# Conditioning weights scaled on ScalarE and summed on VectorE, and six more gate jobs by seven products

## What is computed

```python
# first stack                                   # second stack
g, u = jnp.split(h @ w_up[i], [D_FF], -1)       m = jax.nn.silu(c) @ ada_w[i] + ada_b[i]
g = depthwise_conv_centered(g, ffn_conv_w[i],   shift1, scale1, gate1, shift2, scale2, gate2 = split(m, 6)
                            ffn_conv_b[i])      u = causal_dwconv(h @ w_up, conv_w, conv_b)
x = x + (jax.nn.silu(g) * u) @ w_down[i]        gate, val = jnp.split(u, 2, -1)
                                                y = (jax.nn.silu(gate) * val) @ w_down
```

## Time and profile before

| | us |
|---|---|
| median of three runs | 2414.7 (2414.57 to 2418.11) |
| the profiled execution | 2417.73 |
| its span, first to last instruction | 2416.0 |
| TensorE, VectorE, ScalarE, GpSimd busy | 2392.8, 1589.2, 714.3, 154.6 |
| granted TensorE clock | 0.998 of full |

### The profile page before, as it was taken

One profiled execution on the slowest core, in us unless ns is written; L12 is line 12 of the kernel. 1 busy time (PEld: TensorE's weight loads), 2 busy tenths in 40 slices (PEclk: granted clock), 3 DMA queues, 4 the chain that ended last, 5 costly groups with the idle time before them and its releaser, 6 DMA issues.

```text
span 2416.0 us, 41407 instructions
## 1 busy us (share of the span) xinstructions
PE 2392.8 (99%) x17196; PEld 2180.2 (90%) x17196; DVE 1589.2 (66%) x3245; ACT 714.3 (30%) x1436; POOL 154.6 (6%) x268
## 2 busy tenths in 40 slices
PE   9999999999999999999999999999999999999998
PEld 7879999987899998999998899997889999889998
DVE  6653887566289837688744489954456984327983
ACT  3451210144312121433132233223423331443321
POOL 2000100000021000001000032021000000000000
PEclk9999999999999999999999999999999999999999
DMA  7935985574399746589454399743334555335552
GB/s 220 239 94 180 337 305 188 151 188 114 105 337 314 239 155 183 185 314 310 155 174 136 107 344 313 235 152 120 108 120 149 166 167 168 120 105 170 162 166 97
DMA packets 403269, 458.36 MB, mean 190 GB/s; under 512 B 50751, under 2 KB 374776, under 8 KB 403084
## 3 DMA queue, kind: packets, MB, share of 16 engines
q1 hardware_dynamic: 370098, 340.53, 45.2%
q0 software_dynamic: 29936, 112.73, 12.8%
q10 hardware_dynamic: 3050, 2.46, 0.4%
HBM read 451.48 MB, written 1.29 MB: 187 GB/s over the span
## 4 chain that ended last, share of the span: by engine, by line
PE 94%; DVE 4%; DMA 1%; issue 1%; ACT 0%; POOL 0%; DVEq 0%; SPq 0%; POOLq 0%; ACTq 0%
PE job_bank L994 39%; PE job_bank L1070 27%; PE job_bank L1049 11%; PE mix_bank L1049 4%; PE job_bank L1539 4%; PE mix_bank L1486 1%; PE job_bank L1514 1%; PE mix_bank L1458 1%; DVE sb_arena L2908 1%; PE mix_bank L1500 1%; PE mix_bank L1605 1%; PE mix_bank L1025 0%; PE mix_bank L1830 0%; PE job_bank L1262 0%; DVE sb_arena L2952 0%
## 5 line engine op out<-in xcount | busy, mean ns | idle before, releaser
L994 PE MATMUL job_bank<-sb_h,sb_ring 128*128 128x256 f32 x3616 | 807.1, 380 | 0.4 <-DVE sb_h L3186 0.4
L994 PEld LDWEIGHTS job_bank<-sb_h,sb_ring 128*128 128x128 f32 x3616 | 674.4, 189 | 98.9 <-issue 8.1
L2908 DVE SCALAR_TENSOR_TENSOR sb_arena<-sb_arena,sb_c_act 128x512 f32<-128x512 f32 x336 | 253.0, 753 | 10.6
L3015 DVE SCALAR_TENSOR_TENSOR sb_arena<-sb_arena,sb_par 128x256 f32<-128x256 f32 x440 | 204.4, 506 | 8.8 <-ACT sb_arena L2071 4.9
L1049 PE MATMUL job_bank<-sb_h,sb_ring 128*128 128x128 f32 x1600 | 184.1, 275 | 0.9 <-ACT sb_h L2374 0.9
L1049 PEld LDWEIGHTS job_bank<-sb_h,sb_ring 128*128 128x128 f32 x1600 | 181.2, 192 | 1.3 <-issue 1.1
L1070 PE MATMUL job_bank<-sb_t,sb_ring 128*128 128x128 f32 x1248 | 165.5, 275 | 0.0
L2071 ACT ACTIVATE sb_arena<-sb_arena,sb_par 128x256 f32<-128x256 f32 x220 | 120.2, 593 | 122.4 <-DVE sb_arena L2983 121.1
L1070 PE MATMUL job_bank<-sb_h,sb_ring 128*128 128x128 f32 x1152 | 152.8, 276 | 0.0
L1070 PEld LDWEIGHTS job_bank<-sb_t,sb_ring 128*128 128x128 f32 x1248 | 152.2, 192 | 0.0
L1070 PEld LDWEIGHTS job_bank<-sb_h,sb_ring 128*128 128x128 f32 x1152 | 144.3, 192 | 6.1 <-issue 3.3
(11 more groups left out here) (511 smaller groups left out, 3242.3 us busy)
## 6 DMA issues: line engine op xcount, KB each, us to landing
sb_arena<-in_ada_w POOLq DMA_DIRECT2D x96, 1024.0 KB, 7.4
sb_ring<-in_ffn_w_up SPq DMA_DIRECT2D x88, 1024.0 KB, 5.2
sb_ring<-in_w_up SPq DMA_DIRECT2D x44, 1024.0 KB, 6.4
sb_ring<-in_ffn_w_down SPq DMA_DIRECT2D x32, 1024.0 KB, 5.1
sb_ring<-in_w_in SPq DMA_DIRECT2D x24, 1024.0 KB, 6.2
sb_ring<-in_w_down SPq DMA_DIRECT2D x16, 1024.0 KB, 5.3
sb_ring<-in_hg_w_in SPq DMA_DIRECT2D x16, 1024.0 KB, 5.5
sb_ring<-in_ml_w_up SPq DMA_DIRECT2D x16, 1024.0 KB, 5.5
```

Of the source, the lines that this page charges most:

```text
L994: mm = pe.matmul(o, st, mv, start=(k0 + k == 0 and t == 0), stop=(k0 + k == kn - 1), skip_group_check=True)
L2908: ins = vec.scalar_tensor_tensor(out=o, in0=w, scalar=col, in1=o, op0=ALU.mult, op1=ALU.add)
L3015: ins = vec.scalar_tensor_tensor(out=o, in0=fraw[:, i % 2, v, j:j + T], scalar=pcol(column, (l * FFN_TAPS + j) * width + c), in1=o, op0=AL ...
```

## The change

Each unit of conditioning weights is scaled in place by ScalarE: four copies of 128x512 with a column of silu(c) as scale (`ada_scale`). VectorE then adds two units (128x2048), folds the sum twice (128x1024, 128x512) and writes the result. The two new VectorE parts stand in other places than the halves did: the first add after the gate's other taps, the folds after the product of gate and value. In the tail of the phase the same two parts take the place of two halves. ScalarE has two scalings more at i = 0 and then one in mid-iteration and one at its end. `FAST_PAIRS` becomes one tuple per layer: gates 1 to 10 in layer 0, gates 2, 3, 4, 6, 7, 8, 9 and 10 in layer 1.

```diff
-FAST_PAIRS = (2, 3, 5, 6, 8, 9)
+FAST_PAIRS = (tuple(range(1, FT // 2)), (2, 3, 4, 6, 7, 8, 9, 10))
...
-            return gates[1:] if stack == 1 else [gates[i] for i in FAST_PAIRS]
+            return gates[1:] if stack == 1 else [gates[i] for i in FAST_PAIRS[l]]
...
+            def ada_scale():
+                u = ada_n[0]
+                act.wait_ge(ada_in[u % ADA_RING], 16 * (u // ADA_RING + 1))
+                for k in range(4):
+                    w = ada_w[:, u % ADA_RING, k, :]
+                    col = u % 2 * 4 + k
+                    ins = act.activation(w, w, ACT.Copy, scale=c_act[:, col:col + 1])
+                ins.then_inc(s.ada_scaled, 1)
+                ada_n[0] += 1
...
                     if g[0] in fast_no:
                         keep_mid(g)
                         gate(i - 1)
+                        ada_scale()
                         keep_corner(g)
                         first_tap(stack, l, i, 0, g)
                     else:
...
                         if i:
                             gate(i - 1)
+                        for _ in range(2 if i == 0 else 1):
+                            ada_scale()
                     if stack == 2:
                         raw_out(stack, l, i, 2, u)
                         first_tap(stack, l, i, 2)
                         if 0 < i <= KD:
                             scale_x(l, i - 1)
+                    ada_scale()
                 gate(FT // 2 - 1)
+                ada_scale()
...
-            def ada_half():
...
-                for k in range(4):
-                    w = ada_w[:, u % ADA_RING, k, :]
-                    col = c_act[:, u % 2 * 4 + k:u % 2 * 4 + k + 1]
...
-                        ins = vec.scalar_tensor_tensor(out=o, in0=w, scalar=col, in1=o, op0=ALU.mult, op1=ALU.add)
...
+            def ada_fold():
+                u, first, second = ada_pair()
+                vec.wait_ge(s.ada_scaled, u + 2)
+                vec.tensor_tensor(second, first, second, ALU.add).then_inc(s.ada_acc, 1)
+
+            def ada_add():
+                u, _, w = ada_pair()
+                own(s.ada_acc, u + 1)
+                step(vec.tensor_tensor(w[:, 0:2, :], w[:, 0:2, :], w[:, 2:4, :], ALU.add))
+                settle()
+                if u + 1 >= ADA_PARTS:
+                    vec.wait_ge(s.ada_summed, (u + 1 - ADA_PARTS) // 4 + 1)
+                o = ada_part[:, u % ADA_PARTS:u % ADA_PARTS + 2, :].rearrange("p u c -> p (u c)")
+                vec.tensor_tensor(o, w[:, 0, :], w[:, 1, :], ALU.add).then_inc(s.ada_acc, 1)
+                ada_n[0] += 2
...
                     if g[0] in fast_no:
                         join_tiles(g, fraw[:, i % 2, 0:2, off:off + T])
-                    ada_half()
                     read_out(vec, g)
                     other_taps(stack, l, i, 0)
-                    ada_half()
+                    ada_fold()
...
                         vec.tensor_tensor(fact[:, 2 * i:2 * i + 2, :], fcv[:, i % 2, 0:2, :], fcv[:, i % 2, 2:4, :],
                                           ALU.mult).then_inc(s.act_ready, 1)
+                    ada_add()
```

More of the change, by code:

```diff
@@ L254, in __init__ @@
         self.x_scaled = sem("x_scaled")
+        self.ada_scaled = sem("ada_scaled")
 def weight_plan(a):
@@ L2129, in layer_x @@
                     modulate_half(n, half, (0, 2, 4), {3 + ns: lambda: tail_squares(jobs_, ns, 1)} if half == 0 else {})
+            ada_n = [0]
+            def ada_scale():
[7 more added lines that the diff above has]
+                ada_n[0] += 1
             def glu(stack, l):
@@ L2887, in _, with ada_pair @@
             ada_n = [0]
-            def ada_half():
+            def ada_pair():
                 u = ada_n[0]
-                vec.wait_ge(ada_in[u % ADA_RING], 16 * (u // ADA_RING + 1))
-                first = u - u % 2
-                if u % 2 == 0 and u + 1 >= ADA_PARTS:
-                    vec.wait_ge(s.ada_summed, (u + 1 - ADA_PARTS) // 4 + 1)
-                o = ada_part[:, first % ADA_PARTS:first % ADA_PARTS + 2, :].rearrange("p u c -> p (u c)")
-                for k in range(4):
-                    w = ada_w[:, u % ADA_RING, k, :]
-                    col = c_act[:, u % 2 * 4 + k:u % 2 * 4 + k + 1]
[L2901 to L2907, removed]
-                        ins = vec.scalar_tensor_tensor(out=o, in0=w, scalar=col, in1=o, op0=ALU.mult, op1=ALU.add)
[L2909 to L2913, removed]
+                return u, ada_w[:, u % ADA_RING, :, :], ada_w[:, (u + 1) % ADA_RING, :, :]
+            def ada_fold():
[8 more added lines that the diff above has]
+                if u + 1 >= ADA_PARTS:
+                    vec.wait_ge(s.ada_summed, (u + 1 - ADA_PARTS) // 4 + 1)
+                o = ada_part[:, u % ADA_PARTS:u % ADA_PARTS + 2, :].rearrange("p u c -> p (u c)")
+                vec.tensor_tensor(o, w[:, 0, :], w[:, 1, :], ALU.add).then_inc(s.ada_acc, 1)
+                ada_n[0] += 2
             def ada_copy():
```

## The result

The changed kernel takes 2431.92 us (median of 4, 2430.93 to 2433.57) against 2415.16 for the kernel before on the same chip: a ratio of 1.0068, 95% interval 1.0055 to 1.0081. The direction held, and the time lies inside the range. The size was 12.9 by the sum and is 16.8.

A forecast was written before the change was run, and what follows sets the result against it. TensorE bounds the kernel, leaving ScalarE 3.35 us for keep_mid. Gains of 3.9 and 1.0 against phase waits of 0.2, 7.3, 2.9 and 7.4 gave +12.9: 2430.6 us, or 2427.6 for the median, range 2411 to 2434.

The forecast's parts named there:

- Scalings stay at 0.61: ScalarE's 384 copies of 128x512: 0.61 us each, 2.45 for a unit of four; bounds 0.40 and 0.71.
- Phase 1: First stack, layer 0: three scaled units end just as TensorE returns; 0.2 us of wait.
- Phase 2: First stack, layer 1: late conditioning weights cost 3.4 us, later GpSimd collisions 2.2 and 1.7; 7.3 in all.
- the step that had been called the weakest: The walk through GpSimd's collisions with VectorE, which gave phase 2's later waits of 2.2 and 1.7 us.
- Phase 3: Second stack, layer 0: start wait 1.7 us, then VectorE's join 1.2 over its limit; 2.9 in all.
- Phase 4: Second stack, layer 1: late form for gate 2 1.3 us, then GpSimd collisions 2.9, 2.6 and 0.6; 7.4 in all.
- The six gates: Second stack, four in layer 0 and two in layer 1: seven products each, 3.9 us less TensorE work.
- VectorE's folds: VectorE's conditioning adds of 128x1024 and 128x512 after scaling: 1.22 and 0.69 us.
- the rule weighed in the prediction: VectorE stands still only for a GpSimd product's length, 1.98 or 1.09 us; sum some 2.5 lower, about 2425.
- A: Rival: scalings stay covered on ScalarE, keep_mid always in time; 2409.8 us, faster; chance 0.16.
- B: Rival: only the phase starts cost, GpSimd's products no longer meet VectorE; +4.5, 2419.2 us; chance 0.23.
- C: Rival: conditioning-weight transfers come late as well, so scalings wait for DMA; some 6 us more, about 2434; chance 0.07.

The follow-up runs named there:

- the start alone: Changed kernel with the third unit's scaling at the first gate moved behind the first Silu; 2424.52 us, 1.0042 of the kernel before.
- the weights first alone: Changed kernel with the first four conditioning-weight transfers of phases 2 and 4 issued before GpSimd's small tap and gate transfers; 2424.49 us, 1.0042 of the kernel before.

## Why the prediction held, and where its sum was short

**Right: the mechanism and nearly every place.** Scalings stay at 0.61; the copies stand behind them; TensorE's waits name `keep_mid`. Point by point against its own steps:

- Phase 1, 0.2: measured 0.16.
- Phase 2: 3.4 at the start, 2.2 and 1.7 later; measured 3.62, 0.49 and 1.48. From the phase's first product to the end of `keep_mid` are 9.87 us, 9.4 by the working, so the earlier trace rows gave the landings well. The walk behind it gave 3.9 where 1.97 came: it is the step that had been called the weakest.
- Phase 3: 1.7 and 1.2; measured 1.51 and 0.88.
- Phase 4: form 1.3, then 2.9, 2.6 and 0.6; measured 2.35, then 2.69, 0.66 and 0.65 with 0.96. The join that decides the 2.69 ends at 1442.61, 13.36 after the end of gate 2's 24 products: 13.3 was worked out. The form was 1.0 later because the second unit landed later: the spacing of 3.1 us taken over from the earlier trace rows is 4.07 here, from 1409.81 to 1413.88. The 2.6 was too much: the walk had left out that after a wait of 2.69 TensorE's frame has moved back as well, so that VectorE's lag meets a later limit. The runs with the start alone and with the weights first alone show the same dependence from the other side.

The waits sum to 15.3 where 17.8 were foreseen. So the sum without its missing terms would have been 10.4, and 16.3 stand in the trace.

**The missing terms.** First, the clock: behind the waits of 3.62 and 2.69 the next 32 products take 5.31 and 5.30 us in place of 3.67, 3.3 in all. The step priced a wait at its length. In these phases no row of the kernel before has a fall of the clock, but its trace has one outside them, at 966 (last section), so this price could have been read ahead. Second, the restart: each of the ten waits costs 0.26 us beyond its own length (the group before it is 0.16 longer from start to start, the first one after it 1.16 in place of 1.06), 2.6 in all; the 0.99 wait of the kernel before had it as well. -4.9 - 0.3 + 15.3 + 3.3 + 2.6 = 16.0, and 16.3 stand in the trace. That the sum came within 4 us is in part luck: 2.5 us of waits too many made up for some of the 5.9 that had no term.

**The gains.** The six gates bring 0.65 each, as foreseen: phase 3 falls from 136.61 to 134.00 for four of them wherever nothing waits. VectorE's folds take 1.22 and 0.69. The 1.22 was 3.67 where it met a GpSimd product of 1.98, L2971 3.01. By the rule weighed in the prediction ("SBUF — State Buffer", Terms, of the Trainium skill: the loser fully blocks) they would be 3.20 and 2.67; the loser waited out the product and 0.3 to 0.5 us more, so the row was rightly preferred.

**Rivals.** A (covered) fell at the first fast gate of phases 2 to 4; what it promised, 2409.8, appears only once the order is mended and the collisions are gone. B (only the starts cost, no collisions) falls twice: the products did meet VectorE, and in the run that takes the large collisions away, +10.6 is left where B had +4.5. C (transfers late as well) was half right: in the steady state one scaling of phase 4 waited 3.48 for its transfer, where nobody waited for ScalarE, but the starts of phases 2 and 4 hung on landings more than the sum had it.

**Open.** What phase 4 would take with the old products if GpSimd's work never met VectorE wasn't tried. Nor is it shown why one wait of 2.35 left the clock alone (below).

## What to carry to other kernels

An engine that is idle 70% of the span still has a place where work costs nothing and one where it costs all: put it behind the operation that others wait for (here Silu, right behind `keep_mid`), never in front, and look at the start of a phase by itself. Where two engines disturb each other, look for the wait that the victim has anyway and let the other's work wait for the event that begins it. And price a wait of the matrix engine above its length, but don't add up waits of one phase: an early one pays for a later one.

## What the runs showed of the hardware that was not expected

**TensorE's clock after a pause.** Over all these runs TensorE's waits above 2.25 us in these phases were 4.05, 3.62, 3.27, 2.71, 2.69, 2.68, 2.35, 2.29 and 2.28. Behind all but the 2.35 the granted clock falls to 0.5 and the products run at half speed for a while (0.21 us from start to start where 0.11 is usual), 1.6 to 1.8 us lost each time; behind 2.23 (twice), 2.17 and all shorter ones of these phases they don't. The kernel before has a fall outside the phases, in the convolution module of the second stack:

```profile
965.01 0.86 PE L1605 MATMUL mix_bank<-sb_arena 128*32 128x128 f32 x22 [1.90 <-issue]
```

TensorE is busy 1.11 of the 2.00 us from 962, stands idle 1.90, and the granted clock is 0.61 from 966 to 968 and 0.54 from 968 to 970. So the length of the wait alone doesn't decide: 1.90 brought a fall and 2.35 none. What else does is open. The Trainium skill, "TensorE: Matmul & The Clock Gate" (What's actually happening), says that the gate knows two rates, half and full: the trace agrees, 0.21 against 0.11.

**A small product of GpSimd can be free or cost 2.4 us.** In the changed kernel a GpSimd product of 1.98 us lengthens VectorE's work by 2.3 to 2.45 us when it meets an addition, and by 0.62 (the taps 2.42 in place of 1.80) when it starts in VectorE's idle 1.23; one of 1.07 costs 1.1 to 1.4, or nothing.
